# Attention weights of the second block: the combine, the normalisation and the squares on GpSimd, tile 3's copies on VectorE

## The chip, the cores and the metric

One Trainium2 chip, one core. The metric is the device time of the slowest core in microseconds; with one core that is this core's time, the median of the runs shown. Besides TensorE (PE), VectorE (DVE), ScalarE (ACT) and GpSimd (POOL) the core has SyncE (SP), which here only starts transfers.

## The reference

The program is two transformer blocks over 512 tokens of width 1024, all in float32. The first block (a mixer of windowed attention, RWKV and gated linear attention) is untouched but for two renamed semaphores. The second puts 16 meta tokens in front (528 tokens) and runs a differential attention, a convolutional feed-forward, an attention over selected keys and another feed-forward. The change lies in the two attentions:

```python
def diff_attention(...):           # 8 heads of 2 x 64
    ...
    def block(start):
        s = jnp.einsum('bqhcd,bkhcd->bhcqk', qb, k)
        s = jnp.where(k_pos[None, :] <= q_pos[:, None], s, -jnp.inf)
        p = jax.nn.softmax(s, axis=-1)
        a = p[:, :, 0] - lam * p[:, :, 1]
        return jnp.einsum('bhqk,bkhe->bqhe', a.astype(v.dtype), v)
    o = sweep_blocks(block, T)
    o = rms_norm(o, subln) * (1.0 - lambda_init)
    return o.reshape(B, T, DA_HEADS * 2 * DA_HEAD_DIM) @ w_o

def dsa_attention(...):            # 16 heads of 64, keys selected by an index score
    ...
        s = jnp.where(valid[:, None], s, -jnp.inf)
        p = jax.nn.softmax(s, axis=-1)
        return jnp.einsum('bhqj,bqjhd->bqhd', p.astype(vs.dtype), vs)
```

## The kernel before

Each engine runs a program of its own, written out by hand; an instruction waits on semaphores, and the queue of an engine is in order. So what sets the order of work is the order of the calls in each engine's function. Weights come through GpSimd's transfer queue into a ring of four slots (`W_RING`), each as a high part and a rest; `high_load(n)` waits until slot n - 4 has been used.

**The differential attention (DA).** 33 units: 8 heads times 4 query tiles n = 0 to 3 (`DA_UNITS`), tile n with (n+1) times 128 keys, and one unit, `(None, 4)`, at place 16 for the last 16 rows of all heads. A unit goes through the engines as follows. TensorE: `scores` for both maps of the head, into one of two pairs of banks. VectorE: `soft`, the negated maximum as a minimum over both maps (L1372). ScalarE: `exps`, the exponentials with their sums (L1099). VectorE: `combine`, a factor from the two sums (L1379, L1380) and then `p0 + factor * p1` over all keys (L1382). TensorE: `transposes` of the combined map into bank 4 or 5 (L739). ScalarE: `copy` of the transposes to SBUF (L1107). TensorE: `values` (L756). When a head is done, VectorE copies its output (`out`, L1392), ScalarE squares it (`square`, L1120), VectorE sums the squares (`square_sums`, L1399); they serve the norm over the head. TensorE's loop runs `scores(v + 3)`, `transposes(v)`, `values(v - 1)`.

**The attention over selected keys (DSA).** 34 units: 8 pairs of heads times 4 query tiles, and two units of last rows at places 16 and 17 (`DSA_UNITS`). `soft` is here an instruction for each head that also adds the mask (L1467), the exponentials are L1154, and VectorE's `normalise` takes the reciprocals (L1474) and multiplies each head's map by its own (L1477, two instructions). `transposes` (L661) write banks 4 and 5, both of them for each unit, so there is one such pair and not two. ScalarE copies both banks at once (L1166), TensorE's `values` are L681, VectorE's `out` is L1488. TensorE's loop runs `scores(v + 3)`, `values(v - 2)`, `transposes(v)`; the transposes of a unit wait for the copy of the unit before:

```python
pe.wait_ge(S["a_prob"], DA_N + v + 1)
pe.wait_ge(S["a_pt"], DA_N + v)
```

VectorE's loop in DSA:

```python
for v in range(N + 2):
    if v < N:
        normalise(v)
    if v + 3 < N:
        soft(v + 3)
    ...
    if v >= 2:
        out(v - 2)
```

`output_rests(8)` makes the rests `o_lo` of the attention's output on GpSimd (L991), after all units' other work on that queue.

## Time and profile before

| | us |
|---|---|
| runs before the change | 1813.02, 1815.38, 1817.6 |
| median | 1815.38 |
| span of the profiled execution | 1816.1 |
| TensorE busy | 1729.2 (95%) |
| VectorE busy | 953.5 (53%) |
| ScalarE busy | 635.5 (35%) |
| GpSimd busy | 334.4 (18%) |

The profile is one execution. Its parts are the busy shares, a table of slices, the groups of instructions by line, the waits, and a timeline; a table of stretches gives the busy time of every engine between two moments, with the clock that was granted to TensorE as a share of 2.4 GHz (0.50 is 1.2 GHz) and the share of the transfer engines. Neighbouring VectorE instructions overlap in the records by up to 0.09 us, so that start to start is the safer measure in a row of them. L12 is line 12 of the kernel before.

### The profile page before, as it was taken

Reading aid. Unit: us, or ns where it says so; the run is one execution under the profiler, and the core shown is the slowest. Engines: PE = TensorE matmul, PEld = TensorE weight load, DVE = VectorE, ACT = ScalarE, POOL = GpSimd, SP = SyncE. Lnnn points to the kernel's source line nnn. Section 1 sums busy time; section 2 is a strip of 40 time slices with the busy share of each in tenths; the row PEclk is TensorE's granted clock in tenths of the full one; section 3 lists DMA queues with packets and bytes.
Section 4 is the critical chain, followed back from the end, with each engine's and each line's share of the span. In section 5 each row is a group of like instructions: output and inputs, shape, how many; then the busy total and the mean of one; then the engine's idle time right before and its main releaser. Section 6 shows DMA issues by size and latency. Waiting matters only on the chain.

```text
span 1816.1 us, 33509 instructions
## 1 busy us (share of the span) xinstructions
PE 1729.2 (95%) x14497; PEld 1558.7 (86%) x14497; DVE 953.5 (53%) x1881; ACT 635.5 (35%) x1098; POOL 334.4 (18%) x454
## 2 busy tenths in 40 slices
PE   6999989979998899999999999999899999999997
PEld 3777779858996589999999999799668999999876
DVE  5237695445335865566552115687884555555003
ACT  3254442343114653222222222322584422222222
POOL 0001012001220012222222222122112222222221
PEclk9999979898998999999999999999999999999999
DMA  8521400126994038898898998789404888888995
GB/s 307 167 81 57 176 2 4 55 58 139 227 205 88 1 77 191 180 183 184 181 181 189 200 197 183 173 192 220 95 2 93 183 183 184 183 182 182 198 205 139
DMA packets 82373, 269.11 MB, mean 148 GB/s; under 512 B 11713, under 2 KB 14785, under 8 KB 82097
## 3 DMA queue, kind: packets, MB, share of 16 engines
q0 software_dynamic: 59616, 217.08, 57.0%
q1 hardware_dynamic: 18736, 44.22, 7.0%
q10 hardware_dynamic: 3872, 5.65, 1.1%
q8 instruction: 115, 1.88, 0.4%
q14 instruction: 34, 0.27, 0.0%
HBM read 254.84 MB, written 2.10 MB: 141 GB/s over the span
## 4 chain that ended last, share of the span: by engine, by line
PE 76%; DVE 6%; DMA 3%; issue 1%; ACT 1%; POOL 0%; ACTq 0%; DVEq 0%
PE banks L595 21%; PE banks L596 20%; PE banks L597 20%; PE banks L2048 3%; DMA w_lo<-in_weights 2%; PE banks L648 1%; PE banks L661 1%; DVE stat L1372 1%; PE banks L681 1%; PE banks L1807 1%; PE banks L1808 1%; PE banks L1809 1%; PE banks L724 1%; PE banks L926 1%; DMA w_hi<-in_weights 1%
## 5 line engine op out<-in xcount | busy, mean ns | idle before, releaser
L595 PE MATMUL banks<-hn_hi,w_hi 128*128 128x264 f32 (+1 forms) x2288 | 655.0, 286 | 16.1 <-DMA w_lo<-in_weights 15.3
L596 PE MATMUL banks<-hn_lo,w_hi 128*128 128x264 f32 (+1 forms) x2288 | 649.0, 284 | 0.0
L597 PE MATMUL banks<-hn_hi,w_lo 128*128 128x264 f32 (+1 forms) x2288 | 648.1, 283 | 0.0
L1023 ACT ACTIVATE w_lo<-w_hi 128x1024 fp32r<-128x1024 f32 x207 | 219.4, 1060 | 793.1 <-DMA w_hi<-in_weights 780.2
L595 PEld LDWEIGHTS banks<-hn_hi,w_hi 128*128 128x128 f32 x2288 | 432.6, 189 | 26.7 <-issue 22.3
L596 PEld LDWEIGHTS banks<-hn_lo,w_hi 128*128 128x128 f32 x2288 | 433.8, 190 | 0.2
L597 PEld LDWEIGHTS banks<-hn_hi,w_lo 128*128 128x128 f32 x2288 | 431.4, 189 | 0.0
L978 POOL DMA_DIRECT2D w_hi<-in_weights x207 | 115.6, 559 | 926.3 <-PE banks L597 850.7
L985 POOL DMA_DIRECT2D w_lo<-in_weights x207 | 182.9, 884 | 156.0 <-ACT w_lo L1023 148.3
L595 PE MATMUL banks<-a_hi,w_hi 128*128 128x264 f32 (+1 forms) x506 | 160.5, 317 | 2.1 <-DVE u_in L1541 0.8
L596 PE MATMUL banks<-a_lo,w_hi 128*128 128x264 f32 (+1 forms) x506 | 160.7, 318 | 0.0
L597 PE MATMUL banks<-a_hi,w_lo 128*128 128x264 f32 (+1 forms) x506 | 160.6, 317 | 0.0
L595 PEld LDWEIGHTS banks<-a_hi,w_hi 128*128 128x128 f32 x506 | 95.3, 188 | 9.7 <-issue 1.3
L597 PEld LDWEIGHTS banks<-a_hi,w_lo 128*128 128x128 f32 x506 | 95.2, 188 | 6.7
L596 PEld LDWEIGHTS banks<-a_lo,w_hi 128*128 128x128 f32 x506 | 95.0, 188 | 6.7
L1274 DVE TENSOR_TENSOR ring_r<-ring,ring_r 128x1024 fp32r<-128x1024 f32 x33 | 40.9, 1238 | 82.7 <-ACT ring_r L1017 82.6
L1808 PE MATMUL banks<-h_r,ring_r 128*128 128x512 f32 x200 | 79.2, 396 | 0.0
L1541 DVE TENSOR_TENSOR u_in<-banks,rs 128x528 f32<-128x528 f32 x44 | 31.2, 709 | 89.4 <-PE banks L597 89.3
L1543 DVE TENSOR_TENSOR u_in<-banks,rs 128x516 f32<-128x516 f32 x44 | 30.6, 696 | 90.1 <-PE banks L597 90.0
L595 PE MATMUL banks<-o_hi,w_hi 128*128 128x264 f32 (+1 forms) x256 | 73.3, 286 | 1.8 <-DMA w_lo<-in_weights 1.3
L596 PE MATMUL banks<-o_lo,w_hi 128*128 128x264 f32 (+1 forms) x256 | 72.5, 283 | 0.0
L597 PE MATMUL banks<-o_hi,w_lo 128*128 128x264 f32 (+1 forms) x256 | 72.4, 283 | 0.0
(419 smaller groups left out, 2708.4 us busy)
## 6 DMA issues: line engine op xcount, KB each, us to landing
w_hi<-in_weights POOLq DMA_DIRECT2D x207, 512.0 KB, 5.1
w_lo<-in_weights POOLq DMA_DIRECT2D x207, 512.0 KB, 7.3
ring<-in_weights SPq DMA_DIRECT2D x50, 512.0 KB, 4.4
arena<-arena SPq DMA_DIRECT2D x80, 66.0 KB, 4.6
arena<-arena ACTq DMA_DIRECT2D x64, 66.0 KB, 5.0
arena<-in_gate_w SPq DMA_DIRECT2D x8, 512.0 KB, 3.5
h<-in_xT SPq DMA_DIRECT2D x2, 1024.0 KB, 6.3
arena<-in_alibi SPq DMA_DIRECT2D x1, 1024.0 KB, 6.9
```

The source lines that it names most:

```text
L595: mm(o, w[0][:, j, :], x[0][:, k, lo:hi], start=first, stop=False)
L596: mm(o, w[0][:, j, :], x[1][:, k, lo:hi], start=False, stop=False)
L597: ins_ = mm(o, w[1][:, j, :], x[0][:, k, lo:hi], start=False, stop=last)
L648: last = mm(psum[:, 2 * (v % 2) + c, 0:keys(n)], qs[r, p, n * P:(n + 1) * P], kz[r, p, 0:keys(n)], start=True, stop=True)
L978: g.dma_start(split_at(n)[0], ins["weights"][n]).then_inc(hi_loaded[w_turn(n)[0]], 16)
L985: g.dma_start(split_at(n)[1], ins["weights"][n], accum_op=ALU.add).then_inc(lo_summed[w_turn(n)[0]], 16)
L1023: nc.scalar.activation(split_at(n)[1], split_at(n)[0].bitcast(F32), ACT.Copy, scale=-1.0).then_inc(S["w_negated"], 1)
L1274: nc.vector.tensor_tensor(ring_lo(n), ring_slot(n), ring_hi(n).bitcast(F32), ALU.subtract).then_inc(S["w_split_d"], 1)
L1541: V.tensor_tensor(halves(u_in[:, g % 4, 2:T2 + 2]), pair(g), rs2, ALU.mult).then_inc(S["u_evac"], 1)
L1543: V.tensor_tensor(halves(u_in[:, g % 4, KEEP + 2:T2 + 2]), kept_pair(g), halves(rs[:, KEEP:T2]), ALU.mult).then_inc(S["u_evac"], 1)
L1808: mm(out, w[0][:, k, :], x_lo, start=False, stop=False)
L2048: last = mm(out(s), lhs[r], rhs[r], start=start, stop=stop)
```

## The change

In DA, VectorE keeps the factor (`factor(v)`, now signalled as `a_inv`), and GpSimd combines: it multiplies the second map by the factor in place, waits for that (`a_scaled`), and adds it to the first. GpSimd also squares the head outputs. In DSA, VectorE keeps the reciprocals (`inverse(v)`) and GpSimd multiplies the two maps; the eight rests `o_lo` are no longer made after all else but in between, after the units in `RESTS_AT`. In both attentions the copy of the transposes goes from ScalarE to VectorE for query tile 3 (`LAST_TILE`) and stays on ScalarE for the others; a second counter, `a_pt_wide`, counts VectorE's copies, and `copied` says which counter and count belong to a unit. Square sums and the first square root come one unit later. Three semaphores of other stages are merged (`meta_in` into `cond_in`, `g_zero` into `zeroed`).

```diff
+    LAST_TILE = 3
+    def copied(units, v, narrow, wide):
+        n = units[v][1]
+        count = sum((m == LAST_TILE) == (n == LAST_TILE) for _, m in units[:v + 1])
+        return (S["a_pt_wide"], wide + count) if n == LAST_TILE else (S["a_pt"], narrow + count)
...
+    RESTS_AT = (22, 23, 24, 25, 27, 31)
...
             def transposes(v):
                 p, n = DSA_UNITS[v]
                 pe.wait_ge(S["a_prob"], DA_N + v + 1)
-                pe.wait_ge(S["a_pt"], DA_N + v)
+                if v:
+                    pe.wait_ge(*dsa_copied(v - 1))
...
+        def da_attention():
+            def combine(v):
+                hd, n = DA_UNITS[v]
+                p0, p1 = (prob(v, c)[:, 0:keys(n)] for c in range(2))
+                pool.wait_ge(S["a_inv"], v + 1)
+                g.tensor_scalar(p1, p1, stat[:, v % 4, 3:4], None, ALU.mult).then_inc(S["a_scaled"], 1)
+                pool.wait_ge(S["a_scaled"], v + 1)
+                g.tensor_tensor(p0, p0, p1, ALU.add).then_inc(S["a_prob"], 1)
...
+                g.tensor_tensor(sq_, x, x, ALU.mult).then_inc(S["hd_sq"], 1)
+            for v in range(DA_N):
+                combine(v)
+                if v - 4 in DA_ENDS:
+                    square(DA_ENDS[v - 4])
+            square(7)
+        def dsa_attention():
+            def normalise(v):
+                p, n = DSA_UNITS[v]
+                pool.wait_ge(S["a_inv"], DA_N + v + 1)
+                for c in range(1 if p is None else 2):
+                    x = dsa_prob(v, c)[:, 0:T2 if p is None else keys(n)]
+                    last = g.tensor_scalar(x, x, stat[:, v % 4, 4 + c:5 + c], None, ALU.mult)
+                last.then_inc(S["a_prob"], 1)
...
+            for v in range(len(DSA_UNITS)):
+                normalise(v)
+                if v in RESTS_AT:
+                    output_rest(RESTS_AT.index(v))
...
             def copy(v):
                 hd, n = DA_UNITS[v]
+                if n == LAST_TILE:
+                    return
                 act.wait_ge(S["a_tr"], v + 1)
...
-                V.scalar_tensor_tensor(out=p0, in0=p1, scalar=s[:, 3:4], in1=p0, op0=ALU.mult, op1=ALU.add).then_inc(S["a_prob"], 1)
+            def copy(v):
+                if DA_UNITS[v][1] != LAST_TILE:
+                    return
+                ve.wait_ge(S["a_tr"], v + 1)
+                if v >= 2:
+                    ve.wait_ge(S["a_pv"], v - 1)
+                V.tensor_copy(pt[:, v % 2, :], psum[:, 4 + v % 2, :]).then_inc(S["a_pt_wide"], 1)
...
             for v in range(DA_N):
-                combine(v)
+                factor(v)
                 if v + 2 < DA_N:
                     soft(v + 2)
+                if v:
+                    copy(v - 1)
...
-                for c in range(heads):
-                    x = dsa_prob(v, c)[:, 0:T2 if p is None else keys(n)]
-                    last = V.tensor_scalar(x, x, stat[:, v % 4, 4 + c:5 + c], None, ALU.mult)
-                last.then_inc(S["a_prob"], 1)
+                V.tensor_copy(pt2[:, v % 2, :, :], psum[:, 4:6, :]).then_inc(S["a_pt_wide"], 1)
...
             for v in range(N + 2):
                 if v < N:
-                    normalise(v)
+                    inverse(v)
                 if v + 3 < N:
                     soft(v + 3)
+                if 0 < v <= N:
+                    copy(v - 1)
...
-        act.wait_ge(S["meta_in"], 16)
+        act.wait_ge(S["cond_in"], 32)
```

The order of the instructions, at three places. First VectorE in DSA, behind the reciprocals of a unit n = 0; the masked minima are the `ISA` rows and belong to the unit three further on. Before:

```order
L1474 RECIPROCAL stat<-stat 128x2 [waits a_exp]
L1477 TENSOR_SCALAR arena<-arena,stat 128x128 [waits dve_step]
L1477 TENSOR_SCALAR arena<-arena,stat 128x128
L1467 ISA arena,stat<-banks,arena 128x512 [waits a_sc,a_tr]
...
L1467 ISA arena,stat<-banks,arena 128x512
...
L1488 COPY arena<-banks 128x128 [waits a_pv]
```

After:

```order
L1539 RECIPROCAL stat<-stat 128x2 [waits a_exp]
L1532 ISA arena,stat<-banks,arena 128x512 [waits a_sc,a_tr]
...
L1532 ISA arena,stat<-banks,arena 128x512
...
L1547 COPY arena<-banks 128x1024 [waits a_pv,a_tr]
L1557 COPY arena<-banks 128x128 [waits a_pv]
```

The two multiplies are gone, and the copy of the transposes of unit n = 3 stands behind both minima of the next unit n = 3. (The small `ISA` rows that read the accumulators are left out.)

Second, VectorE in DA, from the work on a unit n = 3 on; L1372 and L1428 are the minima, the reduction to 128x4 is the square sum. Before:

```order
L1380 SCALAR_TENSOR_TENSOR stat<-arena,stat 128x1 [waits dve_step]
L1382 SCALAR_TENSOR_TENSOR arena<-arena,stat 128x512 [waits dve_step]
L1372 TENSOR_REDUCE stat<-banks 128x2 [waits a_sc]
L1379 RECIPROCAL stat<-arena 128x1 [waits a_exp]
...
L1382 SCALAR_TENSOR_TENSOR arena<-arena,stat 128x128 [waits dve_step]
...
L1399 TENSOR_REDUCE arena<-arena 128x4 [waits hd_sq]
```

After:

```order
L1436 SCALAR_TENSOR_TENSOR stat<-arena,stat 128x1 [waits dve_step]
L1428 TENSOR_REDUCE stat<-banks 128x2 [waits a_sc]
L1435 RECIPROCAL stat<-arena 128x1 [waits a_exp]
...
L1444 COPY arena<-banks 128x512 [waits a_pv,a_tr]
...
L1461 TENSOR_REDUCE arena<-arena 128x4 [waits hd_sq]
```

The combines are gone; the copy of the transposes of the unit n = 3 stands behind the minimum of the unit n = 2, and the square sum a unit later, behind the minimum of the next n = 3.

Third, GpSimd between the loads of the last slots of DA's projection and the first of the output projection. Before, the loads follow one another:

```order
L985 DMA w_lo<-in_weights 128x1024 [waits w_negated]
L978 DMA w_hi<-in_weights 128x1024 [waits slot_used]
```

After, all units stand between them; one head, and the square of the head before it:

```order
L1014 TENSOR_SCALAR arena<-arena,stat 128x128 [waits a_inv]
L1016 TENSOR_TENSOR arena<-arena 128x128 [waits a_scaled]
L1014 TENSOR_SCALAR arena<-arena,stat 128x256 [waits a_inv]
L1016 TENSOR_TENSOR arena<-arena 128x256 [waits a_scaled]
L1014 TENSOR_SCALAR arena<-arena,stat 128x384 [waits a_inv]
L1016 TENSOR_TENSOR arena<-arena 128x384 [waits a_scaled]
L1014 TENSOR_SCALAR arena<-arena,stat 128x512 [waits a_inv]
L1016 TENSOR_TENSOR arena<-arena 128x512 [waits a_scaled]
L1027 TENSOR_TENSOR arena<-arena 128x512 [waits hd_sum,a_o]
```

GpSimd's queue, which held nothing in this stage, now holds two instructions a unit, and the next weight load is behind the last of them.

## Rows read from the trace of the kernel before

**Rows 1.** The page: busy time, share of the span, instructions of TensorE.
```profile
PE 1729.2 (95%) x14497; PEld 1558.7 (86%) x14497; DVE 953.5 (53%) x1881; ACT 635.5 (35%) x1098; POOL 334.4 (18%) x454
```

**Rows 2.** Stretches: bounds, length; busy time of each engine; clock, DMA share, GB/s.
```profile
565.00:645.00 80.00, 69.39 (x533) 44.87 (x532) 63.95 (x151) 54.61 (x176) 0.00 (x0) 0.91 0.04 7
1297.00:1380.00 83.00, 78.65 (x746) 50.08 (x747) 66.00 (x271) 65.51 (x177) 10.39 (x8) 0.97 0.01 3
589.00:597.00 8.00, 7.30 (x57) 4.99 (x56) 7.72 (x19) 6.41 (x21) 0.00 (x0) 1.00 0.00 0
605.00:613.00 8.00, 8.00 (x52) 5.65 (x48) 5.14 (x13) 4.89 (x16) 0.00 (x0) 0.79 0.00 1
```

**Rows 3.** Timeline of DA from the transposes n=3: start, length, engine, line.
```profile
628.17 0.61 PE L739 MATMUL banks<-ident,arena 128*128 128x128 f32 x4
...
629.25 0.68 DVE L1399 TENSOR_REDUCE arena<-arena 128x4 f32<-128x512 f32 x1
...
629.38 1.13 PE L724 MATMUL banks<-arena 64*128 64x512 f32 x4
...
630.76 1.23 DVE L1372 TENSOR_REDUCE stat<-banks 128x2 f32<-128x1024 f32 x1
...
636.12 0.61 PE L739 MATMUL banks<-ident,arena 128*128 128x128 f32 x4
```

**Rows 4.** Timelines of TensorE, ScalarE and VectorE in a pair of DSA.
```profile
1357.73 1.09 PE L661 MATMUL banks<-ident,arena 128*128 128x128 f32 x8
1358.76 1.13 PE L648 MATMUL banks<-arena 64*128 64x512 f32 x4
1359.82 0.88 PE L681 MATMUL banks<-arena 128*64 128x128 f32 x12
1360.62 0.44 PE L661 MATMUL banks<-ident,arena 128*128 128x128 f32 x2
...
1364.02 0.87 PE L661 MATMUL banks<-ident,arena 128*128 128x128 f32 x6
...
1358.86 1.03 ACT L1166 ACTIVATE arena<-banks 128x1024 f32<-128x1024 f32 x1
...
1360.04 0.69 DVE L1467 CUSTOM_DVE_ANT_0 arena<-banks,arena 128x512 f32<-128x512 f32 x1 [0.63 <-PE banks L648]
...
1363.01 0.75 DVE L1477 TENSOR_SCALAR arena<-arena,stat 128x384 f32<-128x384 f32 x2
```

**Rows 5.** VectorE by shape, 560 to 655: count, busy, mean ns, idle before.
```profile
L1372 DVE TENSOR_REDUCE stat<-banks 128x2 f32<-128x1024 f32 x8 | 9.8, 1225 | 2.2 <-PE banks L726 2.0
L1380 DVE SCALAR_TENSOR_TENSOR stat<-arena,stat 128x1 f32<-128x1 f32 x33 | 7.3, 220 | 1.2
L1392 DVE COPY arena<-banks 128x512 f32<-128x512 f32 x8 | 5.5, 683 | 0.7 <-PE banks L756 0.7
...
L1382 DVE SCALAR_TENSOR_TENSOR arena<-arena,stat 128x128 f32<-128x128 f32 (+4 forms) x33 | 18.4, 558 | 1.2
```

**Rows 6.** GpSimd: a memset and one early product by timeline, the later products by line.
```profile
149.61 0.61 POOL L2212 TENSOR_TENSOR arena<-norm_tmp 128x256 f32<-128x256 f32 x1
221.19 1.80 POOL L2219 MEMSET hn_raw<- 128x2048 f32 x1 [70.96 <-PE banks L1809]
...
L2234 POOL TENSOR_TENSOR arena<-arena,lvlmask x10: 1269/1277/1778, 272.1 to 299.5; 128x512 f32<-128x512 f32 x10
```

**Rows 7.** ScalarE's silu and the meta tokens' transfer: ns min/median/max, start.
```profile
L2350 ACT ACTIVATE arena<-arena x1: 1061/1061/1061, 118.0 to 118.0; 128x1024 f32<-128x1024 f32 x1
...
L1754 SPq DMA_DIRECT2D h<-in_metaT x1: 695/695/695, 69.7 to 69.7; - x1
```

**Rows 8.** VectorE beside GpSimd: timeline of two places, and one line's durations.
```profile
149.70 0.54 DVE L2558 TENSOR_TENSOR small<-cols,small 128x2 f32<-128x2 f32 x1
1349.30 1.68 DVE L1477 TENSOR_SCALAR arena<-arena,stat 128x128 f32<-128x128 f32 x2
...
L2558 DVE TENSOR_TENSOR small<-cols,small x16: 160/160/539, 119.1 to 217.0; 128x2 f32<-128x2 f32 x16
```

More of the change, by code:

```diff
@@ L535, in build, with da_copied, dsa_copied @@
     LAST_AT = [v for v, (p, n) in enumerate(DSA_UNITS) if p is None]
+    LAST_TILE = 3
[3 more added lines that the diff above has]
+        return (S["a_pt_wide"], wide + count) if n == LAST_TILE else (S["a_pt"], narrow + count)
+    DA_WIDE = sum(n == LAST_TILE for _, n in DA_UNITS)
+    def da_copied(v):
+        return copied(DA_UNITS, v, 0, 0)
+    def dsa_copied(v):
+        return copied(DSA_UNITS, v, DA_N - DA_WIDE, DA_WIDE)
     def values_done(v):
@@ L1003, in pool_block2 @@
                 g.memset(qlast, 0.0).then_inc(S["zeroed"], 1)
+            if n == S_DAO:
+                da_attention()
             if n == S_DSAO:
-                output_rests(8)
+                dsa_attention()
             high_load(n + W_RING)
@@ L1134, in da_attention @@
                 copy(v)
-                if v - 3 in DA_ENDS:
-                    square(DA_ENDS[v - 3])
-                if v == DA_N - 3:
+                if v == DA_N - 2:
                     root(0, 0, 25)
@@ L1140, in da_attention @@
             high(0)
-            square(7)
             high(1)
@@ L1372, in soft, with factor @@
                     V.tensor_reduce(stat[:, v % 4, 0:2], psum[:, 2 * (v % 2):2 * (v % 2) + 2, 0:keys(n)], AX.X, ALU.min).then_inc(S["a_max"], 1)
-            def combine(v):
+            def factor(v):
                 hd, n = DA_UNITS[v]
@@ L1379, in combine @@
                 st.link(V.reciprocal(s[:, 2:3], e[:, 1:2]))
-                st.link(V.scalar_tensor_tensor(out=s[:, 3:4], in0=e[:, 0:1], scalar=nlam, in1=s[:, 2:3], op0=ALU.mult, op1=ALU.mult))
-                p0, p1 = (prob(v, c)[:, 0:keys(n)] for c in range(2))
-                V.scalar_tensor_tensor(out=p0, in0=p1, scalar=s[:, 3:4], in1=p0, op0=ALU.mult, op1=ALU.add).then_inc(S["a_prob"], 1)
+                V.scalar_tensor_tensor(out=s[:, 3:4], in0=e[:, 0:1], scalar=nlam, in1=s[:, 2:3], op0=ALU.mult, op1=ALU.mult).then_inc(S["a_inv"], 1)
+            def copy(v):
+                if DA_UNITS[v][1] != LAST_TILE:
+                    return
+                ve.wait_ge(S["a_tr"], v + 1)
+                if v >= 2:
+                    ve.wait_ge(S["a_pv"], v - 1)
+                V.tensor_copy(pt[:, v % 2, :], psum[:, 4 + v % 2, :]).then_inc(S["a_pt_wide"], 1)
             def out(hd):
@@ L1473, in normalise, with copy @@
                 ve.wait_ge(S["a_exp"], 2 * DA_N + v + 1)
-                st.link(V.reciprocal(stat[:, v % 4, 4:4 + heads], stat[:, v % 4, 2:2 + heads]))
-                for c in range(heads):
-                    x = dsa_prob(v, c)[:, 0:T2 if p is None else keys(n)]
-                    last = V.tensor_scalar(x, x, stat[:, v % 4, 4 + c:5 + c], None, ALU.mult)
-                last.then_inc(S["a_prob"], 1)
+                V.reciprocal(stat[:, v % 4, 4:4 + heads], stat[:, v % 4, 2:2 + heads]).then_inc(S["a_inv"], 1)
+            def copy(v):
+                if DSA_UNITS[v][1] != LAST_TILE:
+                    return
+                ve.wait_ge(S["a_tr"], DA_N + v + 1)
+                if v >= 2:
+                    ve.wait_ge(S["a_pv"], values_done(v - 2) - (v - 2 in LAST_AT))
+                V.tensor_copy(pt2[:, v % 2, :, :], psum[:, 4:6, :]).then_inc(S["a_pt_wide"], 1)
             def out(v):
@@ L2218, in _ @@
         pool.wait_ge(S["slot_used"], S_IN1 + N_IN1)
-        g.memset(g_at, 0.0).then_inc(S["g_zero"], 1)
+        g.memset(g_at, 0.0).then_inc(S["zeroed"], 1)
         pool.wait_ge(S["s1_out"], 16)
@@ L2610, in g_take @@
             if lv == 0:
-                ve.wait_ge(S["g_zero"], 1)
+                ve.wait_ge(S["zeroed"], 2)
             for hd in range(0, 4, 2):
```

66 lines of the change are left out of this document (35 added, 31 removed).

## Prediction

> **What bounds the kernel now.** I read the page's busy shares first: TensorE is busy for 95% of the span [rows 1], so almost everywhere only TensorE's own work counts. The change touches two short stages, so the second view is the table of stretches [rows 2]. In the differential attention (565 to 645 us, "DA" below) the transfers are at 4% and TensorE is busy 69.4 of 80 us; in the selected attention (1297 to 1380, "DSA") 78.7 of 83. GpSimd does nothing in the first and 10.4 us in the second. Third, the timeline inside one repetition of each stage.
>
> I number a unit by v and its query tile by n = 0 to 3 (keys 128, 256, 384, 512). In DA four units, one head, repeat every 636.12 - 628.17 = 7.95 us [rows 3]. VectorE is the engine without slack: in a steady stretch of 8 us it is busy for 7.72, TensorE for 7.30, ScalarE for 6.41 [rows 2]. In DSA TensorE has no gap at all: transposes, scores, values and the next transposes follow one another without idle time [rows 4]. So in DA work taken from VectorE could pay, up to TensorE's own 7.3; in DSA nothing taken from VectorE or ScalarE can pay in the steady part, and whatever delays TensorE there is lost in full.
>
> **VectorE's relief in DA.** The combine, 33 instructions of 0.56 us mean, leaves VectorE: 2.2 us a head. It takes in one copy of 512 columns from PSUM a head, which by the head output copy costs 0.68 [rows 5]. VectorE's share falls to about 6.4 us a head. ScalarE loses that copy and the square. Neither is worth anything until the longer path below is shown to be shorter than 7.95.
>
> **The combine on GpSimd.** One instruction becomes two with a wait between them: multiply, then add. The add is two-input: the trace has 0.61 us for 256 columns and 1.28 (median of ten) for 512 [rows 6], so about 0.95 for 384. The multiply by a per-partition factor is nowhere in the trace on GpSimd. Its bounds: a memset of 2048 columns takes 1.80 us, or 0.45 for 512, and it only writes; the two-input row gives 1.28. I take the middle, 0.87 for 512 and 0.65 for 384, since it reads one operand, between none and two. The Trainium skill (GPSIMD Engine Reference, 3.1 Elementwise) gives 769 ns for a tight 512-element loop; by that, with 384 columns in proportion, the head below would be 0.17 us shorter and the whole sum 2.3 us smaller; no row here shows it.
>
> Now the cycle that returns after four units. Start it at the transposes of a unit n=3. TensorE: transposes, values of the unit before, scores n=3, until the minimum begins: 628.17 to 630.76, 2.6 us [rows 3]. The minimum over 1024 columns: 1.2. Then the square sum, which the change moves to just behind it: 0.6 net of overlap. The factor (reciprocal and a product, 0.22 the latter [rows 5]): 0.4. Hand-overs: 0.1. Then GpSimd in order: n=2 with 0.65 + 0.95 + 0.1 = 1.7, and behind it n=3 with 0.87 + 1.28 + 0.15 = 2.3, since the factor of n=3 is ready before GpSimd is. Sum 8.9 us against 7.95: the head gets longer by 0.95, though VectorE has become free. Seven intervals make 6.7; the last unit's combine, on the path by itself, adds about 1.4 (2.15 in place of one combine, whose mean over all widths is 0.56, so some 0.75 at 512). DA: **+8.1**. With the memset's rate the two GpSimd steps are 1.4 and 1.9 and DA gains 3.5 us of length; with the two-input price 2.0 and 2.7, and 13.4.
>
> The square on GpSimd (1.3 us a head) stands behind the combine of n=3 and is over before the n=0 unit needs GpSimd; the two n=0 and n=1 units leave it time. Cost nothing; if that cover is gone it is 1.3 a head, inside the rival on locks. The copy of tile 3 on VectorE waits for transposes that come a GpSimd step later; values of n=3 need it only after scores n=3 and transposes n=0, 2.3 us on: nothing.
>
> **The wide copy in DSA.** Here the order matters. In DSA one pair of banks takes every unit's transposes, so the transposes of unit v+1 wait for the copy of unit v. Before, ScalarE starts that copy for n=3 at 1358.86, right behind the transposes, and is done at 1359.89; TensorE meanwhile runs scores and values and reaches the next transposes at 1360.62, so there is 0.7 to spare [rows 4]. After, VectorE's copy is queued behind both masked minima of unit v+4, also n=3. Those need scores that TensorE only starts at 1358.76; they begin at 1360.04 and take 0.69 each, 1.23 together net of the overlap of neighbours, so the copy can begin at 1361.27. It reads 1024 columns from PSUM; the minimum over as many takes 1.23 [rows 5], so it ends at 1362.5. The next transposes start at 1362.55 in place of 1360.62: TensorE stands for **1.93 us**, with nothing to fill it because its queue is in order. Six pairs have this form: 11.6. The pair followed by the two last-row units has a 256-column unit in between: 1.3, an estimate. The last pair has no minimum in front; copy 1.22 for 1.03: 0.2. Together +13.1.
>
> **The normalisation in DSA.** Two multiplies a unit move to GpSimd. The tight unit is n=2: VectorE starts its two at 1363.01 and ends at 1363.76, TensorE's transposes start at 1364.02, 0.26 later [rows 4]. GpSimd: 2 x 0.65 + 0.1 = 1.4, to 1364.4: 0.4 late, eight times: **+3.2**. At the memset's rate 0.8, which fits: 0. At the two-input price 2.0: 1.0 late, and n=3 another 0.4: 11. The rests o_lo, already on GpSimd, are now placed among the multiplies; before they blocked VectorE's multiplies instead. I put this at no change.
>
> **Without weight.** ScalarE's silu now waits for the meta tokens too: issued at 69.7, while the silu runs at 118.0 [rows 7]. The memset's semaphore is only renamed. GpSimd's weight loads behind each attention wait in any case for slots that the output projection frees afterwards. The waits of da_output on two copy counters are for copies already done.
>
> **Sum.** The profiled span is 1816.1, 0.7 above the median of 1815.38. 1816.1 + 8.1 + 13.1 + 3.2 = 1840.5, less the 0.7: **1840**. Ends of the multiply alone: 1832 and 1853.
>
> **Rival 1, locks.** At 149.61 GpSimd runs a two-input op of 0.61 [rows 6]; VectorE's product of two 128x2 operands, issued at 149.70, takes 0.54 in place of the 0.16 median and ends when GpSimd has. VectorE's pair of 128-column multiplies at 1349.30, beside GpSimd's subtractions, takes 1.68, more than the 0.75 of a pair of 384 columns [rows 4, 8]. The factor's product in DA has two SBUF operands and is issued while GpSimd combines the unit before. In my cycle it meets the last part of that add and GpSimd would be busy anyway. If it meets whole instructions, at n=2 and n=3, each up to 1.28, or the square gets in between, the head grows by another 1.5 to 2: +12, **1852**. For: it is shown. Against: most of it falls in time that GpSimd's queue takes already. The Trainium skill (SBUF — State Buffer, Who interferes with whom) says that a VectorE instruction with two SBUF inputs and a GpSimd one that reads SBUF exclude each other for the whole instruction; by that rule, the trace agrees. DSA's masked minima have one SBUF input and PSUM, and show no stretching.
>
> **Rival 2, the clock.** After the gaps around the last-row unit the granted clock fell: 0.79 over 605 to 613 [rows 2], which is 3.4 of 8 us at 1.2 GHz and costs half of that, 1.7 us. A stall of 1.9 at each DSA pair might do this each time: 7 x 1.7 = 12, **1852**. Against: in steady DA, with TensorE idle for 0.7 of 8 us, the clock stays at 1.00.
>
> **Rival 3, faster.** DA follows TensorE's 7.3 instead: 7 x 0.65 = 4.5 off. It decides at the two GpSimd steps: 8.9 less 4.0 leaves 4.9, so n=2 and n=3 together must take under 3.0; the two adds alone take 2.2. And the wide copy must find VectorE ahead of TensorE, which the order in the diff excludes: the minima need scores behind the transposes. Both together: **1811**. Only the first, with the DSA stall: 1825.
>
> **Rival 4, the wide copy stalls but DA stays even**: 1829 to 1832.
>
> **Chances.** Forecast with its own range 1832 to 1848: 0.55. Locks 0.12, clock 0.15, rival 4 and milder forms 0.10, rival 3 and no change 0.08. Range **1828 to 1858**. A measurement can tell about 0.3% (5.4 us) from none. Faster 0.03, same 0.04, slower 0.93.
>
> **What would show it.** In DSA: a TensorE gap of 1.9 in front of the n=0 transposes, released by a VectorE 128x1024 copy that starts 2.4 us behind the end of the n=3 transposes; period 8.53 to about 10.9. In DA: a head of 8.9, VectorE idle, transposes of n=3 released by GpSimd's add; the multiply at 0.87. If the copy starts right behind the transposes the DSA step is wrong; if the multiply takes under 0.5, DA is nearly even; if the 0.22 product lasts over 0.8 often, rival 1; a granted clock below 0.9 in DSA, rival 2.

## The result, and the profile after

The changed kernel takes 1874.93 us (median of 4 runs, 1872.25 to 1880.65) against 1816.49 before in the same rounds: ratio 1.0336, 95% interval 1.0311 to 1.0360. The forecast was 1840 with a range to 1858, so the direction was right and the loss, 58 us, was over twice the 24 forecast. The profiled spans are 1871.6 and 1816.1 us.

The page's first part of the kernel after:

```profile
PE 1748.4 (93%) x14497; PEld 1568.9 (84%) x14497; DVE 929.9 (50%) x1798; ACT 619.5 (33%) x1073; POOL 479.0 (26%) x595
```

Against [rows 1], GpSimd has 145 us more and TensorE's instructions are the same number. The first product of DA's output projection starts at 663.43 in place of 649.43 us. So the kernel after is 14 us behind when DA ends (it entered DA 1.4 us ahead), and the rest of the 55.5 us of span is lost behind it, in DSA. These stretches of the kernel after lie in the two stages (the columns are those of [rows 2]):

```profile
586.73:596.87 10.14, 7.67 (x54) 5.01 (x55) 6.10 (x16) 5.34 (x19) 8.70 (x10) 1.00 0.00 0
...
1339.67:1353.92 14.25, 10.22 (x78) 6.50 (x77) 5.96 (x25) 6.13 (x21) 8.55 (x8) 0.88 0.00 1
1297.00:1425.00 128.00, 92.99 (x753) 59.12 (x751) 61.39 (x235) 60.54 (x174) 77.43 (x73) 0.87 0.09 19
```

The first is one DA head: 10.14 us where it was 7.95, with GpSimd busy for 8.70 of it and no clock lost. The second is one DSA pair: 14.25 where the prediction counted from 8.53, at a granted clock of 0.88. The third shows that the clock was low over the whole stage (0.87 against 0.97 in [rows 2]).

The whole of DSA, from the first transposes to the first product of the output projection, in the kernel before (first row) and after:

```profile
1301.42:1377.34 75.92, 72.64 (x717) 46.24 (x717) 62.48 (x254) 60.97 (x165) 9.06 (x7) 1.00 0.01 2
```

```profile
1316.11:1434.08 117.97, 87.18 (x716) 54.92 (x716) 47.48 (x196) 53.08 (x155) 79.29 (x71) 0.85 0.00 1
```

The stage is 42 us longer. TensorE idles for 30.8 us in place of 3.3, which is 27.5, and the same products take 87.2 us in place of 72.6 at a granted clock of 0.85, which is 14.5.

GpSimd in DA by shape (count, busy us, mean ns, idle before), from 560 to 656 us, which leaves out the last squares. L1014 is the new multiply by a factor per row, L1016 the sum, L1027 the square:

```profile
L1014 POOL TENSOR_SCALAR arena<-arena,stat 128x512 f32<-128x512 f32 x8 | 12.5, 1566 | 3.0 <-DVE stat L1436 2.7
L1016 POOL TENSOR_TENSOR arena<-arena 128x512 f32<-128x512 f32 x8 | 10.1, 1263 | 0.7
L1014 POOL TENSOR_SCALAR arena<-arena,stat 128x384 f32<-128x384 f32 x8 | 9.9, 1244 | 7.7 <-DVE stat L1436 7.7
L1016 POOL TENSOR_TENSOR arena<-arena 128x384 f32<-128x384 f32 x8 | 8.0, 995 | 0.7
...
L1027 POOL TENSOR_TENSOR arena<-arena 128x512 f32<-128x512 f32 x6 | 6.3, 1043 | 0.0
```

The sum costs what [rows 6] said. The multiply, with fewer operands to read, costs more than the sum: 1.57 us for 512 columns, where the prediction took 0.87 and 1.28 as the upper bound.

The timelines of TensorE, VectorE and GpSimd in one DSA pair of the kernel after, to be read against [rows 4]:

```profile
1341.77 0.69 DVE L1532 CUSTOM_DVE_ANT_0 arena<-banks,arena 128x512 f32<-128x512 f32 x1 [2.19 <-PE banks L666]
...
1342.99 1.22 DVE L1547 COPY arena<-banks 128x1024 f32<-128x1024 f32 x1
...
1344.36 0.62 PE L680 MATMUL banks<-ident,arena 128*128 128x128 f32 x2 [1.94 <-DVE arena L1547]
1344.91 0.80 PE L666 MATMUL banks<-arena 64*128 64x128 f32 x4
1345.64 1.97 PE L700 MATMUL banks<-arena 128*64 128x128 f32 x16
...
1350.63 0.87 PE L680 MATMUL banks<-ident,arena 128*128 128x128 f32 x6 [1.31 <-POOL arena L1042]
...
1353.71 1.09 PE L680 MATMUL banks<-ident,arena 128*128 128x128 f32 x8 [0.78 <-POOL arena L1042]
...
1348.11 5.55 POOL L1042 TENSOR_SCALAR arena<-arena,stat 128x384 f32<-128x384 f32 x4 [1.71 <-DVE stat L1539]
```

The wide copy (L1547) stands behind the two minima, and TensorE waits 1.94 us for it. Behind that wait its products run slowly: the 16 of L700 take 1.97 us, against 1.09 for the same 16 at 1361.41 in the kernel before. Then come 1.31 and 0.78 us of waiting for the multiplies of tiles 2 and 3. The table of waits of DSA, 1310 to 1437 us (us in total, times, longest), adds them up:

```profile
PE banks L680 <- POOL arena L1042: 18.5, 19, 2.1
...
PE banks L680 <- DVE arena L1547: 11.7, 6, 1.9
```

These are nearly all of the 30.8 us that TensorE idles in the stage. The other 14.5 us of the stage's loss are no wait: they are products at the lower clock.

### The profile page after: what moved, and what is told of

Same layout as the page of the kernel before. It is cut to its first block, busy times and chain, and to the rows that moved or that the text cites. A ratio compares the mean times of both kernels' runs of the same rounds, so it can differ in the third digit from the quotient of the medians.

```text
span 1871.6 us, 33541 instructions
## 1 busy us (share of the span) xinstructions
PE 1748.4 (93%) x14497; PEld 1568.9 (84%) x14497; DVE 929.9 (50%) x1798; ACT 619.5 (33%) x1073; POOL 479.0 (26%) x595
## 4 chain that ended last, share of the span: by engine, by line
PE 74%; DVE 5%; POOL 5%; DMA 2%; issue 1%; ACT 1%; DVEq 0%; ACTq 0%; POOLq 0%
PE banks L613 20%; PE banks L614 20%; PE banks L615 20%; PE banks L2119 3%; POOL arena L1042 2%; DMA w_lo<-in_weights 2%; POOL arena L1014 1%; PE banks L666 1%; PE banks L680 1%; PE banks L1878 1%; PE banks L1880 1%; PE banks L1879 1%; POOL arena L1016 1%; PE banks L743 1%; PE banks L947 1%
## 5 line engine op out<-in xcount | busy, mean ns | idle before, releaser
L1042 POOL TENSOR_SCALAR arena<-arena,stat 128x128 f32<-128x128 f32 (+4 forms) x66 | 71.7, 1102 | 44.4 <-DVE stat L1539 44.4
```

What stands on the lines that cost most here:

```text
L1042: last = g.tensor_scalar(x, x, stat[:, v % 4, 4 + c:5 + c], None, ALU.mult)
```

## The experiments

Theory: the multiply's price (T1) and the copy's place (T2) make the loss, and a lower clock behind the waits adds to both (T3). Rivals: VectorE and GpSimd exclude each other (the prediction's locks), or the hand-over to another engine costs what it costs whatever the instruction. In the diffs, `DA_LAST_TILE` and `DSA_LAST_TILE` name the tile whose copy VectorE makes, 99 for none. Where a text says "the kernel before" with an edit, the merged semaphores and the new place of the rests `o_lo` among the units (`RESTS_AT`) are in it too; wide_copy_first and short_two below, at 1.0005 of before, show that these cost nothing that can be measured.

**The two halves.** All of the change in one stage, the other as before.

```diff
 # da_only: DSA as before
+    DA_LAST_TILE = 3
+    DSA_LAST_TILE = 99
 # dsa_only: the other way round
+    DA_LAST_TILE = 99
+    DSA_LAST_TILE = 3
```

> The differential attention (DA) changed, the selected attention (DSA) as in the kernel before. Theory P (price: GpSimd's multiply takes 1.57 us at 512 columns, and the two stages only add): DA alone is longer by what the trace after shows, about 14 us, so 1816 + 14 = 1830, and nothing outside the stage moves. Rival L (the stages disturb each other, or the loss comes from contention that both parts are needed for): less than 8 us here and less than 30 in DSA alone, with the rest only when both are there.

> DSA changed, DA as in the kernel before. Theory P: +41 us, 1857, with a period of 14.25 us a pair as in the kernel after. Rival L: clearly less than 41.

Measured: 1836.7 us (ratio 1.0107, interval 1.0084 to 1.0131) and 1857.95 us (1.0242, 1.0215 to 1.0269). Against 1817.01 before that is 19.7 and 40.9, together 60.6, which is the 58.4 of the whole within the intervals. The times of the stages add up. da_only is above the 1830 that was expected: its profiled execution came to DA 3.0 us ahead of that of before, lost 18.9 us in DA, and another 5.4 between DA and DSA, where the program is the same and the kernel after lost nothing. What made these 5.4 is open.

**DSA's two edits apart.**

```diff
 # wide_copy_only: multiplies on VectorE as before, only
+    DSA_LAST_TILE = 3
 # multiply_only: copies on ScalarE as before, only
-                    last = V.tensor_scalar(x, x, stat[:, v % 4, 4 + c:5 + c], None, ALU.mult)
+                    last = g.tensor_scalar(x, x, stat[:, v % 4, 4 + c:5 + c], None, ALU.mult)
```

> Of the whole change only this is left: in DSA the copy of tile 3's transposes is VectorE's, behind both minima of the next unit of tile 3. Multiplies on VectorE, DA as before. My prediction's step: 6 stalls of 1.93, one of 1.3, 0.2, so +13 and 1829, with the clock at 1.00. If the gap also costs TensorE's clock, as the 0.88 in the kernel after hints, about 1.4 more for each stall: +23, 1839. Rival: VectorE, relieved of nothing here, is later still and the period goes beyond 12.

> In DSA only the normalising multiplies (and the placing of the rests o_lo) are on GpSimd; all copies on ScalarE, DA as before. Theory P: a pair needs 2 x (0.61 + 0.92 + 1.25 + 1.57) = 8.7 us of GpSimd and up to 1.3 for a rest; tile 2 is 1.6 late, tile 3 another 0.9, tile 1 about 1: a period of 11.5 to 12.2 in place of 8.53, +24 to +30, so 1840 to 1846. Rival (my prediction's price of 0.65 and 0.87 was right and the trace's 1.57 is time in which VectorE holds the shared port): with VectorE's wide copies gone the multiplies of 512 columns take under 1.2 and the time is under 1830.

Measured: 1836.66 us (1.0111, 1.0095 to 1.0127), so 19.7 for the copy; and 1850.9 us (1.0186, 1.0171 to 1.0201), so 33.9 for the multiplies, more than the 24 to 30 expected from the trace, where the prediction had 3.2 and at most 11. TensorE's timeline of multiply_only:

```profile
1328.01 0.66 PE L681 MATMUL banks<-ident,arena 128*128 128x128 f32 x4 [1.10 <-POOL arena L1039]
...
1330.45 0.87 PE L681 MATMUL banks<-ident,arena 128*128 128x128 f32 x6 [0.79 <-POOL arena L1039]
...
1333.77 1.09 PE L681 MATMUL banks<-ident,arena 128*128 128x128 f32 x8 [1.00 <-POOL arena L1039]
```

Three tiles of a pair wait, not the one that the prediction called tight: 2.9 us a pair. The table of waits has 24.2 us of TensorE waiting for GpSimd, 21 times. Over the stage it reads:

```profile
1301.17:1409.41 108.24, 84.89 (x717) 53.91 (x717) 38.30 (x188) 60.80 (x163) 79.38 (x71) 0.86 0.00 1
```

TensorE idles for 23.3 us in place of 3.3, and its products take 12.3 us more at a clock of 0.86. Together the two edits would be 53.6; in dsa_only they cost 40.9, with 17.3 us of waits for GpSimd in place of 24.2. It fits that TensorE's stop for the copy gives GpSimd time to catch up; no run tests this by itself.

**The copy's place, and the clock.** Two changes to wide_copy_only: the copy written ahead of the minima; and, in the other, eight products that nobody reads put where TensorE stands for the copy.

```diff
 # wide_copy_first
-                if v + 3 < N:
-                    soft(v + 3)
                 if 0 < v <= N:
                     copy(v - 1)
+                if v + 3 < N:
+                    soft(v + 3)
 # wide_copy_filled, in front of TensorE's wait for the copy
+                if v and DSA_UNITS[v - 1][1] == DSA_LAST_TILE:
+                    for _ in range(8):
+                        nc.tensor.transpose(psum[:, 7 - v % 2, 3 * P:4 * P], ident[:, :], ident[:, :])
```

> The kernel in which only the last query tile's turned weights of the DSA attention are copied by VectorE (1836.7 us), with the copy written ahead of the two minima (of the unit three on) instead of behind them. P (the 1.95 us in front of the next transposes are two minima, 0.6 to 0.8 us, that stand ahead of the copy, and the copy's 1.22 us against ScalarE's two halves): the copy is done about 0.6 to 1.2 us earlier and the stall shrinks to 0.7 to 1.2 us; the minima come 1.2 us later, but these scores are needed three units on. Time 1824 to 1829. Rival (it is the copy on the path whatever its place, and the minima behind it start a stall of their own): 1834 or more.

> The kernel in which only the last query tile's turned weights of the DSA attention are copied by VectorE (1836.7 us), with eight matrix products more on TensorE ahead of each set of transposes that follows such a copy: they turn the identity into a part of a PSUM bank that nobody reads, some 8 x 0.22 = 1.8 us of work in the place of the 1.95 us wait. Nothing else of the computation changes. P (the part of the excess over the six stalls of 1.95 us is the clock: after each wait TensorE runs some microseconds at half clock, in the 40 us stretches 0.87, 0.96 and 0.83 where the kernel before had 0.91, 1.00 and 1.00): the granted clock of these stretches is back near 1.0, and the time falls by 4 to 7 us, to 1830 to 1833. Rival (the copies cost what they cost by waits alone, and the clock is chance): the time stays at 1836 to 1838, or rises.

Measured: wide_copy_first 1818.65 us (12 runs; 1.0005, 0.9990 to 1.0020). That is better than the 1824 to 1829 expected: the whole 19.7 us are gone within the interval, and TensorE idles for 4.3 us in DSA against 3.3 before. So the copy cost nothing by itself and everything by the line it was written on. wide_copy_filled 1829.63 us (1.0061, 1.0045 to 1.0077), 7.0 less than without the filling. The wait, filling included, is as long as it was: the filling and what is left of the wait make 1.92 us.

```profile
1321.98 1.09 PE L675 MATMUL banks<-ident 128*128 128x128 f32 x8
1323.90 0.44 PE L684 MATMUL banks<-ident,arena 128*128 128x128 f32 x2 [0.83 <-DVE arena L1565]
```

The granted clock of wide_copy_only (first two rows) and wide_copy_filled (last two), by stretch:

```profile
1320.00:1360.00 40.00, 34.03 (x352) 21.22 (x352) 31.03 (x114) 23.43 (x69) 3.63 (x3) 0.96 0.01 2
1360.00:1400.00 40.00, 33.65 (x260) 23.36 (x261) 24.24 (x85) 18.84 (x51) 6.75 (x6) 0.83 0.00 1
```

```profile
1320.00:1360.00 40.00, 38.05 (x398) 24.24 (x397) 31.93 (x119) 23.76 (x72) 3.24 (x3) 1.00 0.01 2
1360.00:1400.00 40.00, 35.77 (x326) 27.19 (x325) 26.19 (x89) 20.25 (x54) 8.62 (x8) 1.00 0.04 10
```

With the work in the waits the clock is 1.00 in both stretches and these us come back. T3 is shown for this kernel: of the copy's 19.7 us, 7.0 were TensorE's clock, and the rest, 12.7, the waits, which the prediction had put at 13.1. The traces of the whole stage agree: TensorE idles 12.0 us more in wide_copy_only than before, and its products take 81.9 us in place of 72.6; in wide_copy_filled they take 73.8 beside the filling. The lower clock does not follow every wait: behind the 1.95 us that ended at 1321.83 in wide_copy_only the products took what they take in the kernel before.

**The multiply's form.** The same product with two tensor operands, the second the factor repeated along the row; the line shown is that of DSA, and two_input_multiply has the same edit in DA.

```diff
-                    last = g.tensor_scalar(x, x, stat[:, v % 4, 4 + c:5 + c], None, ALU.mult)
+                    last = g.tensor_tensor(x, x, stat[:, v % 4, 4 + c:5 + c].to_broadcast([P, T2 if p is None else keys(n)]), ALU.mult)
```

> The changed kernel (1874.9 us) with every multiply of a weight map on GpSimd written as a product of two tensors, the second being the factor repeated along the row, instead of a product by a scalar per row. P (the price of 606, 925, 1246 and 1568 ns for 128, 256, 384 and 512 columns is that of the instruction's form): the multiplies take what the sum takes, about 455, 726, 995 and 1263 ns; GpSimd has 0.9 us less per DA head, where it is busy 9.05 of 10.15 us, so DA falls by about 7 us, and the DSA pair loses 0.6 us in front of its tiles 2 and 3 each, about 5 us over the stage. Time 1860 to 1866. Rival (any multiply of this kind on GpSimd is slowed by the data it reads, or by the other engines' use of the memory): 512 columns stay at 1.5 us or more, and the time at 1872 or more.

> The kernel in which only the DSA multiplies stand on GpSimd (1850.9 us), with each multiply written as a product of two tensors, the factor repeated along the row. In the two_input_multiply kernel this form took 398, 613, 826 and 1039 ns for 128, 256, 384 and 512 columns, against 606, 925, 1246 and 1568 ns; two of them for each tile save 0.6, 0.8 and 1.05 us on tiles 1, 2 and 3, where TensorE stood 1.10, 0.79 and 1.00 us a pair for them. P (the excess of 33.9 us is the instruction's price and nothing else): a wait of 0.5 us stays in front of tile 1 and of the units around the last rows, and the time is 1823 to 1830. Rival (the excess comes from the hand-over to another engine and from the clock, whatever the multiply costs): 1838 or more.

Measured: the whole change in this form 1857.52 us (1.0217, 1.0192 to 1.0242), 17.4 less than after and less than the 1860 to 1866 expected, which took the multiply to cost what the sum costs; in DSA alone 1830.81 us (1.0087, 1.0058 to 1.0117), 20.1 less than multiply_only. GpSimd in DA of two_input_multiply:

```profile
L1015 POOL TENSOR_TENSOR arena<-arena,stat 128x512 f32<-128x512 f32 x8 | 8.3, 1039 | 3.6 <-DVE stat L1437 3.1
...
L1015 POOL TENSOR_TENSOR arena<-arena,stat 128x384 f32<-128x384 f32 x8 | 6.6, 826 | 10.8 <-DVE stat L1437 10.7
```

1039 ns in place of 1566, and cheaper than the sum of two full maps (1263). So the price of a multiply was that of the instruction's form, not of memory traffic or of the other engines: over 512 columns either form lasts the same within 1%, whatever the other engines do beside it (1562 to 1576 ns in the kernel after, 1033 to 1043 here). T1 holds for the 17.4 us. It is not all of the multiplies' cost: in DSA alone 13.9 us are left, a little above the 1823 to 1830 expected for the time. In the trace of multiply_two_input TensorE idles 10.5 us more in the stage than before and its products take 3.8 us more, at a clock of 0.96. The hand-over is late even so.

**Both mended.** The changed kernel with the two-tensor form and the copy first.

> The changed kernel (1874.9 us) with both causes that the runs found taken out: the multiplies on GpSimd as products of two tensors (that alone: 1857.5 us) and in DSA the wide copy written ahead of the minima of the unit three on (that alone, in a kernel with nothing else changed, took the time from 1836.7 to 1818.7 us). P (these two are the whole of the loss in DSA but for the 14 us that multiply_two_input keeps; DA keeps its longer loop, 9.29 us a head, some 11 us): 1840 to 1847. Rival (in the full change the copy waits for GpSimd's late multiplies anyway, so that its place is worth little): 1851 or more.

Measured: 1845.88 us (1.0153, 1.0126 to 1.0180), within what was expected, and 29 less than after. The change remains a loss of 27 to 28 us without its two mistakes: about half of its 58 us were in its idea.

**DA's edits apart.**

```diff
 # da_rest_only: squares on GpSimd, tile 3's copy on VectorE, combination on VectorE
+                V.scalar_tensor_tensor(out=p0, in0=p1, scalar=s[:, 3:4], in1=p0, op0=ALU.mult, op1=ALU.add).then_inc(S["a_prob"], 1)
 # da_combine_only: squares and copies on ScalarE as before
+                    A(osq[:, 0:4, :], otok[:, 0:4, hd * P:(hd + 1) * P], ACT.Square).then_inc(S["hd_sq"], 1)
+    DA_LAST_TILE = 99
```

> The kernel before with two edits in the DA attention alone: GpSimd squares the head outputs, and VectorE copies tile 3's turned weights; the combination stays on VectorE and DSA is as before. These are the two steps that the prediction took at nothing. VectorE, the bound of a DA head at 7.95 us, then has a copy of 512 columns (0.68 us) more, so here they must cost about 0.5 us a head: P: 1820 to 1824. What would speak against it: 1819 or less (VectorE was not the bound), or 1828 or more (GpSimd's square of 1.04 us locks VectorE's products of two tensors out, as it did once in the outputs_on_scalar kernel, where a combination of 128 columns took 1.09 us in place of 0.35).

> The kernel before with the DA combination alone on GpSimd, in the changed kernel's form (multiply by a scalar per row, then sum); square and copies stay on ScalarE, DSA is as before. da_only took 19.7 us more than before, da_rest_only 7.8. P (a head is the loop through GpSimd that the prediction named, and the combination alone makes it): the square sum is still in the loop and GpSimd's two steps are 2.3 and 2.9 us, so a head stays at 9.6 to 10.1 us and the time is 1831 to 1835; the rest adds little to it, since VectorE is no longer full. Rival (the two halves add up): 19.7 less 7.8, that is 1829 or less.

Measured: 1824.66 us (1.0054, 1.0033 to 1.0074), 7.8 more than before, and 1833.02 us (1.0078, 1.0057 to 1.0099), 14.3 more. A head takes 9.19 and 9.69 us. The medians nearly add up to da_only's 19.7, which is what the rival said; the heads do not (1.24 and 1.74 more, against 2.19 together), and the two intervals are too wide to decide between them. The first kernel shows the lock on VectorE plainly:

```profile
634.42 1.04 POOL L1028 TENSOR_TENSOR arena<-arena 128x512 f32<-128x512 f32 x1 [8.14 <-DVE arena L1455]
```

```profile
634.45 1.03 DVE L1435 SCALAR_TENSOR_TENSOR stat<-arena,stat 128x1 f32<-128x1 f32 x1
635.52 0.75 DVE L1437 SCALAR_TENSOR_TENSOR arena<-arena,stat 128x512 f32<-128x512 f32 x1
```

The factor's product of one column, 0.22 us otherwise, takes 1.03 and ends with GpSimd's square. It does so in each of the three steady heads from 619 to 646. With 0.81 for the lock and 0.68 for the copy, less the 0.3 that VectorE had idle, a head is 1.2 longer: the 1.24. This is a sum of read parts; no run has the square or the copy alone.

**Is VectorE the bound of a DA head?** Candidates, each the kernel before with an edit in DA.

```diff
 # outputs_on_scalar: ScalarE copies head outputs, GpSimd squares them
+                A(otok[:, 0:4, hd * P:(hd + 1) * P], psum[:, item_bank(hd), :].rearrange("p (n m) -> p n m", n=4), ACT.Copy).then_inc(S["a_o"], 1)
 # short_two (tiles 0 and 1), short_one (tile 0): combination on GpSimd
+                g.tensor_tensor(p1, p1, stat[:, v % 4, 3:4].to_broadcast([P, keys(n)]), ALU.mult).then_inc(S["a_scaled"], 1)
+                pool.wait_ge(S["a_scaled"], k)
+                g.tensor_tensor(p0, p0, p1, ALU.add).then_inc(S["a_prob_short"], 1)
 # scores_earlier: TensorE's scores of tile 3 ahead of the values of tile 2
-                if v + 3 < DA_N:
+                if v + 3 < DA_N and v + 3 not in EARLY:
                     scores(v + 3)
                 if v < DA_N:
                     transposes(v)
+                if v + 4 in EARLY:
+                    scores(v + 4)
                 if v:
                     values(v - 1)
```

> A candidate: the kernel before with two edits in the DA attention alone. GpSimd squares the head outputs (in the changed kernel this took 1.04 us a head there), and ScalarE, which has their 0.9 us free, copies the head outputs out of PSUM in VectorE's place; the combination stays on VectorE, and DSA is as before. P (VectorE is the bound of a DA head, 7.95 us, and its output copy of 512 columns is 0.6 to 0.7 us of it): a head takes 7.3 to 7.5 us and the time is 1811 to 1814. Rival (ScalarE, with a copy that waits for the values in front of its exponentials, becomes late for VectorE): same or slower, 1817 to 1825.

> A candidate: the kernel before, with the DA combination of the two short tiles (128 and 256 columns) on GpSimd, as a product with the factor repeated along the row (0.40 and 0.61 us) and a sum (0.46 and 0.73 us); everything else as before. In the trace of before, 1.9 and 2.2 us lie between the start of these combinations on VectorE and TensorE's transposes of the same unit, against 1.6 and 1.1 us on GpSimd, and VectorE loses 0.84 us of its 7.72 in 7.95 us a head. P (VectorE is the bound and short products hide on GpSimd): a head takes 7.4 to 7.6 us and the time is 1811 to 1815. Rival (GpSimd's two-tensor operations lock VectorE's products of two tensors out, or ScalarE's chain sets the head): 1816 or more.

> The same candidate with the DA combination of tile 0 alone (128 columns) on GpSimd: VectorE loses 0.35 us a head. P: 1814 to 1816.5; a head takes 7.6 to 7.8 us. Rival (as for the two short tiles): the same as before, 1817 to 1819.

> The kernel before with one edit in the order of TensorE's DA work: the scores of tile 3 stand ahead of the values of tile 2 (0.83 us) instead of behind them. The loop of a head in the trace of before: TensorE from the scores of tile 1 to the end of the scores of tile 3 5.0 us without a gap, then the minimum (0.2 later, behind a combination, and 1.23 long), the two exponentials 1.4, and the scores of tile 1 again; sum 7.95. Their bank is free, by the exponentials of tile 1, at 636.74 against the scores' start at 637.33. P (the loop bounds the head, not VectorE's load): the loop loses 0.5, but VectorE is then the bound at 7.72 us: a head takes 7.7 to 7.8 us, and the time is 1815 to 1816.5. Rival (the head stays at 7.95, as something else sets it): 1817 to 1818.

> A candidate to beat both kernels: the edit of scores_earlier, and the DA combination of the two short tiles on GpSimd (short_two, which alone changed nothing: 1817.0 against 1816.9 us). P: the loop is 7.3 to 7.5 us a head, VectorE has 6.9, TensorE 7.3: 1812 to 1814. Rival (the values of tile 2, now later, hold up ScalarE's copy and the head outputs, or VectorE's two-tensor products are locked out by GpSimd's): 1816 or more.

| kernel | us (12 runs each) | ratio, interval | head, us |
|---|---|---|---|
| outputs_on_scalar | 1820.98 | 1.0015, 0.9999 to 1.0031 | 7.95 |
| short_one | 1818.02 | 1.0009, 0.9992 to 1.0026 | 7.96 |
| short_two | 1816.99 | 1.0005, 0.9990 to 1.0021 | 7.96 |
| scores_earlier | 1817.16 | 0.9999, 0.9984 to 1.0015 | 7.84 |
| scores_earlier_short | 1813.41 | 0.9976, 0.9960 to 0.9992 | 7.59 |

Three edits took work off VectorE, a shorter head was expected of each, and the steady head did not move. The head of before and that of short_two, by stretch:

```profile
629.38:637.33 7.95, 7.25 (x55) 4.94 (x55) 7.66 (x19) 6.40 (x23) 0.00 (x0) 1.00 0.01 2
```

```profile
628.00:635.96 7.96, 7.26 (x56) 4.95 (x55) 6.84 (x17) 6.41 (x23) 2.20 (x4) 1.00 0.01 2
```

VectorE falls from 7.66 to 6.84 us and the length stays. The head is a loop. TensorE works from the scores of tile 1 to the end of the scores of tile 3 without a gap (4.9 us, with what lies between), VectorE takes the minimum of tile 3 (1.23), ScalarE its two exponentials (1.4), and the next scores of tile 1 go into the same banks; with the hand-overs that is 7.95 us. It shows as the one gap of a head in TensorE's timeline of before:

```profile
633.52 0.70 PE L724 MATMUL banks<-arena 64*128 64x256 f32 x4 [0.70 <-ACT arena L1099]
```

Only when the loop was shortened did VectorE's load matter. scores_earlier alone gives nothing in time that can be measured, which is what its rival said; its steady head is 7.84 from one start of tile 3's scores to the next, and 7.6 to 8.0 by other instructions. With both edits the head is 7.59 by each instruction, and the kernel is 5.3 us faster than its rounds' 1818.7 (1.5 to 7.3 us by the interval). Seven heads that are 0.36 shorter make 2.5 us; where the rest comes from is not shown. The expected head of 7.3 to 7.5 was missed by a little: TensorE now waits 0.23 us for the exponentials ahead of the scores of tile 3.

## Why the prediction was right in direction and wrong in size

The forecast's terms were 8.1 us for DA, 13.1 for the copy, 3.2 for the multiplies in DSA and nothing for the clock. Measured alone they are 19.7, 19.7 (7.0 of it clock) and 33.9, less 12.7 that the last two share. The multiply's price is the step that failed first, and not the only one: with the cheaper form, 1.04 us for 512 columns, the change still loses about 40 us where 24 were forecast.

- **What bounds the kernel now.** DSA right: TensorE without a gap, nothing to gain. DA wrong: "VectorE is the engine without slack" was read from 7.72 busy of 8 us. VectorE had 4% idle, but the loop through all three engines set the length, as short_two shows. The mistake did not touch the forecast's sum; it made "work taken from VectorE could pay" and rival 3's 4.5 us too hopeful.
- **The multiply on GpSimd**: the step that failed. It measured 1.57 and 1.24 us for 512 and 384 columns, against 0.87 and 0.65 taken. It is in two terms of the sum, DA and the normalisation. The reason given (it reads one operand, so it lies between none and two) was an order that the engine does not keep; both ends of the range came from other instructions, and the true price was beyond both. By the figure of the Trainium skill (GPSIMD Engine Reference, 3.1 Elementwise) it would have been 0.77 for 512; no multiply of this form over 512 columns took under twice that here.
- **The DA cycle**: right as a mechanism. With the measured steps (2.31 and 2.95 us in place of 1.7 and 2.3) the prediction's own list sums to 10.2 us, and the head is 10.14. Seven intervals and the last unit then make 15.3 + 2.1 = 17.4, where 8.1 stood; da_only shows 19.7. With the prices of the two-tensor form the list sums to 9.3, and the head of two_input_multiply is 9.29. In the traces DA lasts 100.2 us from its first scores to the output projection, against 84.8 before and 80.6 to 84.1 in five other kernels with DA unchanged, so one pair of traces tells the loss only to some 4 us. (Two slips of the sums: the low end for DA, 3.5, comes to 2.7 by its own terms, which makes 1831 of the 1832, and VectorE's share comes to 6.2 a head in place of 6.4; the profile has 6.10. The forecast hangs on neither.)
- **Square and copy of tile 3 for nothing**: in the changed kernel their place in the loop was counted; in front of a full VectorE they are not free (da_rest_only, 7.8 us). The prediction named the lock as the price if the cover goes; in da_rest_only the lock is 0.81 us a head, and the copy is most of the rest.
- **The wide copy, 1.93 us a pair**: right, 1.94 measured, six times, 11.7 us in sum, and 1.41 for the pair in front of the last-row units, estimated at 1.3. Cause right too: moving the copy ahead of the minima removes it.
- **The normalisation, 3.2 (0 to 11)**: failed twice. The price made it 1 us later at tile 2, and the step "the tight unit is n=2" was too narrow: with a multiply pair of 1.8 to 3.1 us tiles 1 and 3 wait as well. Measured alone 33.9 us; of these 20.1 go with the instruction's form. What is left, 13.9, is over twice the 6 us that the prediction's own reckoning (0.26 of slack, tile 2 alone) gives for 0.83 us a multiply, so the reckoning failed too, and not only the price.
- **Without weight**: the kernels that have these edits and little else run at 1.0005 of before. The rests' new place cost nothing either.
- **Rival 1, locks**: the mechanism occurs and is small. In DA of the changed kernel 7 of 33 factor products are stretched, by 4.1 us in all, and the head's length is accounted for without them. One beside a sum, and one beside a multiply of the form by a scalar, VectorE's rows:

```profile
582.61 1.05 DVE L1436 SCALAR_TENSOR_TENSOR stat<-arena,stat 128x1 f32<-128x1 f32 x1
```

```profile
592.54 0.22 DVE L1436 SCALAR_TENSOR_TENSOR stat<-arena,stat 128x1 f32<-128x1 f32 x1
```

  and GpSimd's of the same moments:

```profile
582.65 0.99 POOL L1016 TENSOR_TENSOR arena<-arena 128x384 f32<-128x384 f32 x1
...
591.61 1.25 POOL L1014 TENSOR_SCALAR arena<-arena,stat 128x384 f32<-128x384 f32 x1 [1.11 <-DVE stat L1436]
```

- **Rival 2, the clock**: true, at 7.0 us for the copy's seven waits where it was priced at 12, and it came on top of the forecast, not in its place. The sign that was named for it, a clock below 0.9 in DSA, is there: 0.85, and 14.5 us of slower products in the stage, since the waits for the multiplies count too. It should have been a term of the sum.
- **Rivals 3 and 4**, a faster or an even DA, did not occur: both needed GpSimd's two steps to be short, and they took 5.3 us. By the prediction's own list under 3.0 would have kept the head even, and TensorE's 7.3 wanted 2.4.

The range ended at 1858 since each of these was held to be the only thing that could go wrong. Clock and multiply went wrong together.

## What to carry to other kernels

An operation moved to another engine has no known price until a row shows this form of instruction on that engine: give the unknown a range that leaves the neighbours' values on both sides, or look for a form that the trace has. In an in-order queue the place of a copy sets what it costs: 19.7 us or none with the same instructions. A busy share of 96% (VectorE, 7.72 of 8 us) does not make an engine the bound: follow the one gap of the busiest engine back until the loop closes, and shorten the loop first; the relief pays only then.

## What the runs showed of the hardware

- GpSimd's multiply of a float32 map by a factor per row takes 606, 925, 1244 and 1566 ns for 128, 256, 384 and 512 columns (the kernel after); written as a product with a repeated column 398, 613, 826 and 1039 ns (two_input_multiply); the sum of two full maps 455, 726, 995 and 1263 ns.
- The exclusion of VectorE and GpSimd goes by GpSimd's instruction too. VectorE's product of two SBUF operands was held to the end of a GpSimd two-tensor operation (1.05 us in place of 0.22 at 582.61 in the kernel after), and ran at 0.22 us beside the multiply by a scalar per row, in each of the 7 overlaps with it alone in DA of that kernel. The Trainium skill (SBUF — State Buffer, Who interferes with whom) has the lock for any GpSimd instruction that reads SBUF; by these rows the measurement decides otherwise for this form.
- With a wait of TensorE of 1.9 us in nearly every pair of DSA the granted clock over the stage was 0.89 (wide_copy_only) against 1.00 before. 56 products that nobody reads, put into the waits, brought it to 0.98 and gave back 7.0 us.
